# Norm weights multiplied into key, value, query and router weights in a two-layer hybrid encoder kernel

## The reference

```python
def rms_norm(x, w):
    y = x * lax.rsqrt(jnp.mean(x * x, axis=-1, keepdims=True) + EPS)
    return y * w

h = x
hn = rms_norm(h, attn_norm_w[0]); h = h + gated_deltanet(hn, ...)      # layer 0, mixer
hn = rms_norm(h, ffn_norm_w[0]);  h = h + swiglu(hn, w_gate, w_up, w_down)
kv = rms_norm(h, kv_norm_w) @ w_kv                                     # keys, values: 4 heads of 64 each
hn = rms_norm(h, attn_norm_w[1]); q = (hn @ w_q) * 64 ** -0.5          # 16 heads of 64
h = h + softmax_with_sinks(q @ k.T + bias, window) @ v @ w_o           # layer 1, mixer
hn = rms_norm(h, ffn_norm_w[1])
logits = hn @ router_w                                                 # 8 experts
top_logit, top_idx = lax.top_k(logits, 2); gate = softmax(top_logit)
h = h + sum over the 2 chosen experts of gate * swiglu(hn, expert weights)
out = rms_norm(h, final_norm_w)
```

## Time and profile before

| what | value |
|---|---|
| time, median of 3 | 1517.67 us (1516.85 to 1518.12) |
| the profiled execution's own time | 1520.69 us |
| its span | 1518.6 us |
| PE busy | 1476.2 us, 97% |
| DVE busy | 1122.0 us, 74% |
| ACT busy | 895.4 us, 59% |
| POOL busy | 94.7 us, 6% |
| mean HBM traffic | 288 GB/s |

### The profile page before, as it was taken

One profiled execution on the slowest core, in us unless ns is written; L12 is line 12 of the kernel. 1 busy time (PEld: TensorE's weight loads), 2 busy tenths in 40 slices (PEclk: granted clock), 3 DMA queues, 4 the chain that ended last, 5 costly groups with the idle time before them and its releaser, 6 DMA issues.

```text
span 1518.6 us, 22634 instructions
## 1 busy us (share of the span) xinstructions
PE 1476.2 (97%) x8983; PEld 1236.9 (81%) x8983; DVE 1122.0 (74%) x1058; ACT 895.4 (59%) x851; POOL 94.7 (6%) x64
## 2 busy tenths in 40 slices
PE   6999999999989989999999999999999999999998
PEld 6988958999977578788888888888888888888886
DVE  4765355455433478888898888988888988889796
ACT  4540134344324346777776777777777777677674
POOL 2330010000000000000000000000000000000000
PEclk9999999999999989999999999999999999999999
DMA  7541027555553169999999999999999999999993
GB/s 256 185 150 57 12 86 233 170 190 182 193 206 112 56 223 373 384 371 379 394 380 374 395 377 371 391 376 363 386 373 373 392 387 359 375 383 376 381 391 123
DMA packets 194334, 437.97 MB, mean 288 GB/s; under 512 B 5280, under 2 KB 28096, under 8 KB 194160
## 3 DMA queue, kind: packets, MB, share of 16 engines
q1 hardware_dynamic: 189248, 423.64, 75.9%
q0 software_dynamic: 2736, 9.24, 2.4%
q10 hardware_dynamic: 2304, 4.43, 0.8%
HBM read 429.41 MB, written 7.88 MB: 288 GB/s over the span
## 4 chain that ended last, share of the span: by engine, by line
PE 82%; DVE 6%; DMA 5%; ACT 4%; issue 2%; POOL 1%; DVEq 0%; SPq 0%; ACTq 0%; POOLq 0%
PE bank L1502 22%; PE bank L1504 22%; PE bank L1503 22%; DMA weights<-in_moe_w_down 2%; DVE weights_lo L1166 2%; PE bank L1538 2%; PE bank L1861 2%; PE bank L1920 2%; PE bank L1729 2%; DVE ws L984 1%; PE bank L2035 1%; DMA weights<-in_moe_w_up 1%; ACT qkv_hi L635 1%; ACT weights_hi L755 1%; DMA weights<-in_a_w_in 1%
## 5 line engine op out<-in xcount | busy, mean ns | idle before, releaser
L1166 DVE TENSOR_TENSOR weights_lo<-weights,weights_hi 128x2048 fp32r<-128x2048 f32 (+1 forms) x396 | 823.2, 2121 | 143.9 <-ACT weights_hi L755 143.3
L755 ACT ACTIVATE weights_hi<-weights 128x2048 fp32r<-128x2048 f32 (+1 forms) x396 | 685.4, 1781 | 266.4 <-DMA weights<-in_moe_w_up 99.9
L1502 PE MATMUL bank<-weights_hi,expert_x_hi 128*128 128x512 f32 x896 | 355.0, 396 | 1.4 <-DVE expert_x_lo L1380 1.1
L1504 PE MATMUL bank<-weights_hi,expert_x_lo 128*128 128x512 f32 x896 | 349.4, 390 | 0.0
L1503 PE MATMUL bank<-weights_lo,expert_x_hi 128*128 128x512 f32 x896 | 349.3, 390 | 0.0
L1502 PE MATMUL bank<-weights_hi,hidden_hi 128*128 128x512 f32 x520 | 204.4, 393 | 2.2 <-DVE hidden_lo L1204 2.2
L1504 PE MATMUL bank<-weights_hi,hidden_lo 128*128 128x512 f32 x520 | 202.6, 390 | 0.0
L1503 PE MATMUL bank<-weights_lo,hidden_hi 128*128 128x512 f32 x520 | 202.5, 390 | 0.0
L1504 PEld LDWEIGHTS bank<-weights_hi,expert_x_lo 128*128 128x128 f32 x896 | 168.2, 188 | 36.4
L1502 PEld LDWEIGHTS bank<-weights_hi,expert_x_hi 128*128 128x128 f32 x896 | 168.3, 188 | 35.8 <-DVE expert_x_lo L1380 1.2
L1503 PEld LDWEIGHTS bank<-weights_lo,expert_x_hi 128*128 128x128 f32 x896 | 168.5, 188 | 33.4
(11 more groups left out here) (311 smaller groups left out, 1514.3 us busy)
## 6 DMA issues: line engine op xcount, KB each, us to landing
weights<-in_moe_w_down SPq DMA_DIRECT2D x56, 2048.0 KB, 10.0
weights<-in_moe_w_up SPq DMA_DIRECT2D x56, 2048.0 KB, 10.0
weights<-in_moe_w_gate SPq DMA_DIRECT2D x55, 2048.0 KB, 9.8
weights<-in_a_w_in SPq DMA_DIRECT2D x8, 2048.0 KB, 9.1
weights<-in_ffn_w_up SPq DMA_DIRECT2D x11, 1024.0 KB, 5.4
weights<-in_ffn_w_gate SPq DMA_DIRECT2D x11, 1024.0 KB, 5.4
weights<-in_ffn_w_down SPq DMA_DIRECT2D x11, 1024.0 KB, 4.9
weights<-in_a_w_out SPq DMA_DIRECT2D x2, 2048.0 KB, 7.7
```

What stands on the lines that cost most here:

```text
L755: act.activation(hi[:, j * n:(j + 1) * n], slot[k][:, j * n:(j + 1) * n], ACT.Copy).then_inc(w_hi[k], 1)
L1166: dve.tensor_tensor(to[:, c], slot[k][:, c], hi[:, c].bitcast(F32), ALU.subtract).then_inc(w_lo[k], 1)
L1502: pe.matmul(dst, ah, bh, start=start, stop=False, skip_group_check=True)
L1504: return pe.matmul(dst, al, bh, start=False, stop=stop, skip_group_check=True)
```

## The change

Norms 2 and 3 become one. DVE multiplies the rows by their root alone; the weights of the norms are multiplied into the weight matrices by ACT, in place, 128 rows of the matrix at a time (`fold`). For this the three weight vectors are loaded as columns, through the transposition of the convolution weights. The transposed rows of norm 2 also serve the queries. The transposes of tile 1 go ahead of the values of tile 0.

For the router, PE transposes the rows `h` themselves; the router's weights are multiplied by the norm's weights on DVE, and the logits by the root. The normalised rows `xn` are still made for the experts, of tile 1 after its `top_two`. The last output products of tile 1 are split in two groups of four, with the router product of tile 0 between. The first expert product waits for the first half of the gathered rows, then for the second.

```diff
+        wcol = view(sm, 832, 3, KT)
-        NATIVE = {0: 0, 2: 1, 3: 2, 4: 3}
+        NATIVE = {0: 0, 2: 1, 4: 2}
 # POOL, at the start
+            for i, w in enumerate((ins["kv_norm_w"], ins["attn_norm_w"][1], ins["ffn_norm_w"][1])):
+                pool.dma_start(convrow[96 + KT * i:96 + KT * i + KT, :],
+                               w.rearrange("(k p) -> k p", p=P)).then_inc(s_small, 16)
 # ACT
-            row_load(2)
-            row_load(3)
+            row_load(4)
+            row_load(5)
...
-            for t in range(NT):
-                squares(2, s_h, 4, [t])
-                turned(2, [2 * t])
+            def fold(i):
+                act.wait_ge(loaded[i], 16 * (PRE_A[i] + 1))
+                for kt in range(KT):
+                    a = act.activation(g8[i][:, kt, :], g8[i][:, kt, :], ACT.Copy, scale=wcol[:, min(i, 1), kt:kt + 1])
+                a.then_inc(s_fold, 1)
+
+            act.wait_ge(s_cw, 1)
+            fold(0)
+            squares(2, s_h, 4, [0])
+            turned(2, [0])
+            squares(2, s_h, 4, [1])
+            fold(1)
+            turned(2, [2])
+            fold(2)
...
-            turned(3)
-            row_load(4)
-            row_load(5)
 # DVE
+                if k == 2:
+                    for q in range(2):
+                        c = slice(q * 512, (q + 1) * 512)
+                        dve.tensor_scalar(xn[:, t, c], h[:, t, c], rs[:, r, t:t + 1], None, ALU.mult).then_inc(s_xn, 1)
+                    return
...
+            link(dve.tensor_copy(wcol.rearrange("p a k -> p (a k)"), bank[7][:, 96:96 + 3 * KT]))
...
-            dve.wait_ge(s_tp, 12)
-            norm_xn(3)
+            dve.wait_ge(s_router, 16)
+            dve.tensor_tensor(router[:, :, :], router[:, :, :], wide(wcol[:, 2, :], E), ALU.mult).then_inc(s_cw, 1)
...
-                link(dve.tensor_copy(logit[:, t, :], bank[4][:, t * 8:t * 8 + 8]))
+                dve.wait_ge(s_rstd, 2 * rstd_of(4) + t + 1)
+                link(dve.tensor_scalar(logit[:, t, :], bank[4][:, t * 8:t * 8 + 8], rs[:, rstd_of(4), t:t + 1], None,
+                                       ALU.mult))
...
-            for t in range(NT):
-                add_h(t, s_aw, 0, (0, 1, 2, 3), 8)
-                norm_x(4, t)
-                if t:
-                    top_two(0)
-                turned(4, [t])
+            add_h(0, s_aw, 0, (0, 1, 2, 3), 8)
+            turned(4, [0])
+            norm_x(4, 0)
+            add_half(1, 0, s_aw, 0, (0, 1, 2, 3))
+            top_two(0)
+            add_half(1, 1, s_aw, 0, (0, 1, 2, 3))
+            turned(4, [1])
             top_two(1)
+            norm_x(4, 1)
 # PE
-                        pe.wait_ge(s_xn, 4 * k + 2 * t + q + 1)
+                        if k == 4:
+                            pe.wait_ge(s_h, 8 + 2 * t + q + 1)
+                        else:
+                            pe.wait_ge(s_xn, 4 * k + 2 * t + q + 1)
...
+            pe.wait_ge(s_small, 16 * 7)
-            pe.transpose(bank[7][:, 0:96], convrow[0:96, :], ident[0:96, 0:96]).then_inc(s_cwt, 1)
+            pe.transpose(bank[7][:, 0:120], convrow[0:120, :], ident[0:120, 0:120]).then_inc(s_cwt, 1)
...
+            turn(2, [0])
             for t in range(NT):
-                turn(2, [t])
...
-                pe.wait_ge(loaded[0], 16 * (PRE_A[0] + 1))
+                pe.wait_ge(s_fold, 1)
...
                 if t:
                     m.then_inc(s_kmm, 1)
+                else:
+                    turn(2, [1])
...
-            turn(3)
-            ready(3)
             pe.wait_ge(s_vS, 2)
             def query(g):
                 k = 1 + g // 2
                 if g % 2 == 0:
-                    pe.wait_ge(loaded[k], 16 * (PRE_A[k] + 1))
+                    pe.wait_ge(s_fold, k + 1)
...
-            merge(1, range(8), [1])
-            pe.wait_ge(s_router, 16)
+            merge(1, range(4), [1])
+            pe.wait_ge(s_cw, 2)
             for t in range(NT):
                 if t:
+                    merge(1, range(4, 8), [1])
                     turn(4, [1])
...
             def first_gather():
+                pe.wait_ge(s_xn, 4 * 3 + 4)
...
-            def e_proj(k, s, done, free=None):
+            def e_proj(k, s, done, free=None, rows=None):
...
+                    if kt % 4 == 0 and rows is not None:
+                        pe.wait_ge(rows, kt // 4 + 1)
...
-            pe.wait_ge(m_Xl, 2)
-            e_proj(0, 0, m_g)
+            e_proj(0, 0, m_g, rows=m_Xl)
```

More of the change, by code:

```diff
@@ L148, in trunk @@
         cst = sb("cst", [P, consts.shape[1]])
-        sm = sb("sm", [P, 832])
+        sm = sb("sm", [P, 864])
         router = sb("router", [P, KT, E])
@@ L342, in trunk @@
         s_og, s_otp, s_ot = sem("s_og"), sem("s_otp"), sem("s_ot")
-        s_oss, s_orstd = sem("s_oss"), sem("s_orstd")
+        s_oss, s_orstd, s_fold = sem("s_oss"), sem("s_orstd"), sem("s_fold")
         s_wo_mm = sem("s_wo_mm")
@@ L457, in _ @@
             for t in range(NT):
-                sp.wait_ge(s_xn, 4 * 4 + 2 * t + 2)
+                sp.wait_ge(s_xn, 4 * 3 + 2 * t + 2)
                 sp.dma_start(xn_rows[t * P:(t + 1) * P, :], xn[:, t, :]).then_inc(s_rows, 16)
@@ L503, in _ @@
                 for q in range(2):
-                    sp.wait_ge(s_xn, 4 * 5 + 2 * t + q + 1)
+                    sp.wait_ge(s_xn, 4 * 4 + 2 * t + q + 1)
                     sp.dma_start(out[0, t * P:(t + 1) * P, q * 512:(q + 1) * 512],
@@ L592, in _ @@
             link = Chain(act, ach)
-            names = [ins["attn_norm_w"][0:1, :], ins["ffn_norm_w"][0:1, :], None,
-                     ins["attn_norm_w"][1:2, :], ins["ffn_norm_w"][1:2, :], None]
-            names[2] = ins["kv_norm_w"].rearrange("(a n) -> a n", a=1)
-            names[5] = ins["final_norm_w"].rearrange("(a n) -> a n", a=1)
+            names = {0: ins["attn_norm_w"][0:1, :], 1: ins["ffn_norm_w"][0:1, :], 4: ins["ffn_norm_w"][1:2, :],
+                     5: ins["final_norm_w"].rearrange("(a n) -> a n", a=1)}
             def row_load(k):
-                if k >= 2:
-                    act.wait_ge(s_xn, 4 * (k - 2) + 4)
+                if k >= 4:
+                    act.wait_ge(s_xn, 4 * (k - 4) + 4)
                 act.dma_start(rows[k % 2][:, :], names[k].to_broadcast([P, D])).then_inc(s_row[k % 2], 16)
@@ L681, in _ @@
             act.activation(beta, tail[:, :, 0:JP], ACT.Exp, scale=-1.0).then_inc(s_bexp, 1)
-            act.wait_ge(s_small, 16 * 4)
+            act.wait_ge(s_small, 16 * 7)
             act.activation(alog, alog, ACT.Exp).then_inc(s_soft, 1)
@@ L935, in norm_x @@
             def norm_x(k, t):
-                if t == 0:
-                    dve.wait_ge(s_row[k % 2], 16 * (k // 2 + 1))
                 r = rstd_of(k)
+                if t == 0 and k != 2:
+                    dve.wait_ge(s_row[k % 2], 16 * (k // 4 + 1))
                 dve.wait_ge(s_rstd, 2 * r + t + 1)
+                if k == 2:
[3 more added lines that the diff above has]
+                    return
                 for q in range(2):
@@ L992, in _ @@
             dve.wait_ge(s_bexp, 1)
-            dve.wait_ge(s_small, 16 * 4)
+            dve.wait_ge(s_small, 16 * 7)
             tail = view(bank[5], 0, NC, 8)
@@ L1150, in _, with add_half @@
                 gate_out(n)
+            def add_half(t, q, sem_in, base, banks):
+                dve.wait_ge(sem_in, base + 2 * t + q + 1)
+                hs = h[:, t, q * 512:q * 512 + 512]
+                dve.tensor_tensor(hs, hs, bank[banks[2 * t + q]][:, :], ALU.add).then_inc(s_h, 1)
             def add_h(t, sem_in, base, banks, first):
                 for q in range(2):
-                    dve.wait_ge(sem_in, base + 2 * t + q + 1)
-                    hs = h[:, t, q * 512:q * 512 + 512]
-                    dve.tensor_tensor(hs, hs, bank[banks[2 * t + q]][:, :], ALU.add).then_inc(s_h, 1)
+                    add_half(t, q, sem_in, base, banks)
                 dve.wait_ge(s_h, first + 2 * t + 2)
@@ L1474, in turn @@
                             kt = 4 * q + j
-                            m = pe.transpose(bank[6 + q][:, j * P:(j + 1) * P], xn[:, t, kt * P:(kt + 1) * P], ident)
+                            m = pe.transpose(bank[6 + q][:, j * P:(j + 1) * P],
+                                             (h if k == 4 else xn)[:, t, kt * P:(kt + 1) * P], ident)
                         m.then_inc(s_tp, 1)
```

6 lines of the change are left out of this document (3 added, 3 removed).

## The result

| | median us | lowest to highest | runs |
|---|---|---|---|
| before | 1519.32 | 1516.85 to 1523.21 | 11 |
| changed | 1523.06 | 1521.10 to 1526.38 | 11 |

The ratio is 1.0027, 95% interval 1.0020 to 1.0035: the changed kernel is about 4 us **slower**. Forecast was 7.2 us faster. The profiled execution took 1524.43 us (span 1522.3), against 1520.69 (1518.6) before.

What follows compares the result with a forecast made beforehand. PE, holding 82% of the span, was taken as the bound, with the experts at its own pace. Terms of 5.3 and 1.9 us made 7.2 us, taking the median from 1517.67 to 1510.5 us; range 1508.8 to 1513.8.

Steps and rivals of the forecast that it cites:

- the slower one, late multiplications: Key/value stage: first eight ACT weight multiplications end after 420.3 us, delaying everything behind; 1520.4 at 2 us each; chance 0.03.
- Part 1: Key, value and query stage: one transposed copy for keys and queries lets the queries start 5.3 us earlier.
- Part 2: Router stage ahead of the experts: routing from unnormalised rows shortens the path to the first expert product by 1.9 us.
- the up weights' landing binds: Ahead of the experts: ACT waits for up weights landing 8.4 us after M; gathered rows' residuals end at M + 16.2.
- M: End of the last attention-output product, 531.86 us in the trace before; times up to the experts are counted from it.
- rival 1: Whole change: the key/query saving of 5.3 us arrives, the router's part gives nothing; 1512.4 us; chance 0.17.
- Rival 2: First expert products run at the low clock after PE stands still behind the gather; 1511.3 to 1514.5 us; chance 0.14.
- the prediction's slack of 1.5 us: First expert products: about 1.5 us that PE could lose there without delaying the next stage, which DVE sets.
- Sum: Whole kernel: 5.3 + 1.9 = 7.2 us faster, the median becoming 1510.5 us.
- the 1.1 us at M: Before the last four output products: the router product of tile 0, added on PE there, makes M 1.1 us later.

Runs made afterwards that it cites:

- Part 1 alone: Kernel before with only the shared key/query norm and transposed copy, weight multiplications and reordering, old router and addresses (6 in the table); 1514.47 us, ratio 0.9972.
- 5: Changed kernel with its grown table and 32 padding columns ahead of the transposed rows; rows 128 bytes further, work area 256; 1522.08 us, ratio 1.0025.
- kernel 10: Changed kernel with the small-value table at 880 columns, work area 192 bytes further than in the kernel before; 1523.06 us, ratio 1.0037.
- kernel 4: Changed kernel, new columns in unused ones, 32 padding columns ahead of the transposed rows, so rows and work area both 128 bytes further; 1514.60 us, ratio 0.9974.
- kernel 7: Kernel before with only the router's part of the change, addresses as before; 1518.25 us, ratio 0.9998.
- experiment 9: As kernel 7, plus three products that nobody reads on PE between the gather and the first expert product; 1517.48 us, ratio 0.9997.
- kernel 2: Changed kernel with its new columns in unused ones of the table, which keeps its old length, so addresses as before; 1512.56 us, ratio 0.9961.
- kernel 3: Changed kernel with the small-value table at 896 columns, work area 256 bytes from its old place; 1511.94 us, ratio 0.9951.
- 12: Changed kernel, new columns in unused ones, work area and gathered rows both 64 bytes further; 1509.11 us, ratio 0.9936.
- kernel 8: Changed kernel with the small-value table at 848 columns, new columns in unused ones, work area 64 bytes further; 1511.06 us, ratio 0.9957.
- kernel 1: Kernel before with only the small-value table grown by 32 unused columns, moving the work area by 128 bytes; 1532.01 us, ratio 1.0091.
- 11: Changed kernel, work area 256 bytes further than before, gathered rows 128 bytes further inside their own space; 1524.80 us, ratio 1.0039.

## Why the prediction was wrong

- **The step that failed** is the first one: "The experts run at PE's own pace, so every microsecond by which they start earlier reaches the end." It holds PE's pace itself for given, 396 / 390 / 390 ns. The change altered that pace to 401 / 395 / 395 by a line that has nothing to do with its purpose, and 2688 products at 4.6 ns more, 12.4 us, outweigh all that was gained. The prediction priced every instruction that the diff moved, and not the tile that it enlarged. None of its rivals had this in it; the slower one, late multiplications, was far off.
- **Part 1** was right in every step: no hole, multiplications of 0.62 us hidden, norm of 0.44 us. The queries start 5.5 us earlier (forecast 5.3). Part 1 alone gives 4.3 us (2.9 to 5.6) at the end.
- **Part 2** was right in its mechanism (the up weights' landing binds, M + 16.1 to the rows, forecast M + 16.2). In size it is less sure: alone it gives 0.3 us (1.7 faster to 1.1 slower), with both parts against part 1 alone the ratios differ by 0.0011, 1.7 us, which the intervals don't resolve; rival 1 is not excluded. The forecast of 1.9 us lies just outside the first of these, and the single traces show 1.7 us with the clock up. How often the low clock eats it in unprofiled runs stays open.
- **Rival 2** exists, though not in the changed kernel's own profile. Behind waits of 1.68, 2.02, 2.10 and 3.12 us the clock fell to half (kernels 5, 10, 4 and 7), behind waits of 1.07 to 2.54 us in nine other traces it did not: the wait's length alone doesn't tell the two apart. The Trainium skill (TensorE: Matmul & The Clock Gate, HAM oscillation) describes a kernel in which the wait ahead of every burst makes the burst start cold; four traces here agree and the nine don't. The price was some 2.7 us in kernel 7 (experiment 9). In kernel 4 the clock was at half from 540.9 to 544.3 us, over 2.9 us of products; these 1.5 us left no mark (span 1507.1, against 1507.4 in kernel 2, where the clock stayed up), as the prediction's slack of 1.5 us would have it.
- **Sum**: with the pace as it was, 5.9 us (3.8 to 8.0), 7.4 (5.5 to 9.4) and 3.9 us (2.4 to 5.6) in three placements (kernels 2, 3 and 4), against 7.2 forecast. The forecast lies inside the first two intervals and above the third. Why kernel 4 gained less is open; its profiled execution was the fastest of its eight, so the trace doesn't show it.
- **Slips in the working** that change nothing here: at full clock the gather of rival 2 would end at M + 12.1 and not M + 11.4 (6.04 us, of which 4.65 at half clock become 2.3), so PE would stand still 3.4 us and not 4; kernel 7 had 3.12. Rival 1 calls the 1.1 us at M certain and leaves them out of its 1512.4. The lower bound of the forecast is given as 1509.0 and, at the range, as 1508.8.

Some of the scatter between executions is the clock as well. The profiled execution of kernel 3 took 1515.38 us, that of kernel 2 1509.57, with the same products. Of these 5.8 us, 4.7 lie ahead of the first expert product (546.06 against 541.32). Kernel 3's clock in two stretches:

```profile
490.00:500.00 10.00, 10.00 (x58) 5.79 (x57) 4.90 (x23) 4.52 (x20) 0.00 (x0) 0.66 0.01 2
100.00:200.00 100.00, 95.28 (x1559) 85.40 (x1559) 56.68 (x102) 18.21 (x52) 7.28 (x8) 0.98 0.19 65
```

In kernel 2 both are at 1.00. As an estimate from these rows, 10 us at 0.66 lose 3.4 us and 100 at 0.98 some 2.

## What to carry to other kernels

Read a diff for what it does to addresses as well as to instructions: a tile that grows moves every tile behind it. Where one kind of product holds most of the time, compare its mean duration in nanoseconds, by form, before and after, ahead of any search for waits; 5 ns in 2688 instructions is more than a well-made edit gains. Put additions into free columns (kernel 2) or behind the operands of the hot loop (not tried here), and try the distance between a product's two operands as a parameter of its own.

## What was unexpected in the hardware

The time of a product depends on how far the tiles that it reads in SBUF lie apart, modulo 256 bytes. With gathered rows as the loaded operand and rounded weights, 512 columns, as the streamed one:

| distance mod 256 bytes | mean ns, high by high / low weights / low rows | sum of 2688, us | runs that show it |
|---|---|---|---|
| 0 | 396 to 397 / 390 to 391 / 390 to 391 | 1053.4 to 1056.4 | before, 2, 3, 4, 6, 7, 9, 12 |
| 64 | 398 / 392 / 390 | 1058.1 | 8 |
| 128 | 400 to 401 / 394 to 395 / 395 | 1065.8 to 1067.7 | changed, 1, 5, 11 |
| 192 | 401 / 395 / 396 | 1067.9 | 10 |

The sums of kernels 4, 5, 7 and 10 hold some first products at the low clock. Moving both together by 128 bytes (kernel 4) changes nothing to speak of. The time from the first of these products to the end of the span, which leaves out all scatter ahead of it, says the same: 965.7 to 968.7 us at 0 (970.4 in kernel 7, with its low clock), 970.0 at 64, 978.0 to 980.1 at 128, 981.1 at 192.

A second tile in the same traces agrees. The last item's hidden rows (`end_hidden`, 8 products of each kind) lie in the space of the normalised rows, where the same edits give other distances: 192 in the kernel before, 64 in the changed one. Its mixed products take 394 to 396 ns at 192, 391 to 394 at 64, 390 at 0 (kernel 8) and 395 at 128 (kernel 10). So they got shorter by the edit that made the large group longer:

```profile
L1503 PE MATMUL bank<-weights_lo,end_hidden_hi 128*128 128x512 f32 x8 | 3.2, 396 | 0.0
L1530 PE MATMUL bank<-weights_lo,end_hidden_hi 128*128 128x512 f32 x8 | 3.1, 392 | 0.0
```

(before, then changed). The feed-forward products of 256 columns are shorter with the high rows at 64 than at 0 (279 to 282 ns against 283 to 284).

The distance between a product's own two operands is not the whole rule. At 64 the three kinds on gathered rows have the same distance and lose 2.2, 2.5 and 0.4 ns each. The feed-forward product of low rows and high weights has both operands in the work area, always at distance 0, and still takes 283, 282, 281 and 285 ns as the high rows beside it stand at 0, 64, 128 and 192. PE loads one product's operand while another product streams, so a streamed tile and the operand loaded beside it may be the pair that counts; no run separates the two. PE's loads of the gathered rows keep their 188 to 189 ns in all of these, so in the profile it is the streaming part that gets longer. The Trainium skill (SBUF — State Buffer, Operand start alignment) lets a float32 operand start at any multiple of four bytes and says that this is about legality, not speed; all placements here keep to it, and the sum of these products is 12.1 us larger in kernel 1 than in the kernel before. By what mechanism the distance acts is open: I have argued none, and no run here separates the reads of one product from the writes of ACT, DVE and the DMA beside it.
